# Norm weights loaded as rows and turned on TensorE, page-table loads issued by GpSimd, and the sync queue left to x and the projection weights

## What is computed

```
x      = 576 rows of 1024           (512 prompt rows, 64 sample rows)
xn     = x * rsqrt(mean(x*x) + eps) * attn_norm_g
q, k, v, qi, ki, wi, u, ga, gb = split(xn @ w_in)      # w_in: 1024 x 4168
ki     = rope(ki);  new_idx_k = ki
ki_all = [cache_idx_k[page_table], ki]                 # samples: 1024 cached keys, by pages of 128
score  = sum_h relu(qi . ki_all) * wi                  # then the best 128 or 256 keys of each query
o      = attention(q, k, v of the chosen keys)
pool_o = pooling branch of u, scaled by pool_scale
h      = x + (sig(ga) * (o @ W_ba) + sig(gb) * (pool_o @ W_bp)) @ w_out
h      = h + two experts of 32 for each token (RMSNorm with ffn_norm_g before it)
y      = RMSNorm_final(h)
```

## Time and profile before

| | |
|---|---|
| time, median of 3 runs | 1216.53 us (1213.72 to 1216.58) |
| profiled execution, first to last instruction | 1206.4 us |
| its own time | not listed apart: the median less the span is 10.1 us |
| PE busy | 1023.5 us, 85% |
| DVE, ACT, POOL busy | 352.1, 224.8, 172.1 us |
| mean rate of the DMA engines | 234 GB/s |
| mean granted TensorE clock | 0.938 |

### The profile page before, as it was taken

The page is one execution under the profiler, slowest core; times in us unless marked ns, Lnnn a source line. Parts: engine busy times, 40 slices in busy tenths (PEclk is TensorE's granted clock), DMA queues, the critical chain, the costliest instruction groups (busy, mean ns, idle before and its releaser), DMA issues.

```text
span 1206.4 us, 11854 instructions
## 1 busy us (share of the span) xinstructions
PE 1023.5 (85%) x4516; PEld 551.9 (46%) x4516; DVE 352.1 (29%) x754; ACT 224.8 (19%) x478; POOL 172.1 (14%) x257
## 2 busy tenths in 40 slices
PE   3998999999999999999985798878888788777780
PEld 3543444767776565775552334333333333333330
DVE  1048999973332111231233001000000000000006
ACT  4144211223333223200221011001100111001002
POOL 2732451100000120000134101000000000000012
PEclk9999999899999999999996799888997999988995
DMA  6420022421201341953035999999999999999986
GB/s 221 172 70 1 7 90 85 166 81 39 71 1 70 140 154 63 369 230 140 17 122 192 331 357 391 400 397 406 404 401 403 400 405 405 395 399 408 396 357 215
DMA packets 51038, 282.66 MB, mean 234 GB/s; under 512 B 12232, under 2 KB 12952, under 8 KB 36143
## 3 DMA queue, kind: packets, MB, share of 16 engines
q1 hardware_dynamic: 37287, 237.82, 51.0%
q0 software_dynamic: 8592, 35.92, 8.5%
q10 hardware_dynamic: 5120, 8.39, 1.8%
HBM read 267.37 MB, written 14.79 MB: 234 GB/s over the span
## 4 chain that ended last, share of the span: by engine, by line
PE 61%; DVE 18%; issue 8%; DMA 5%; ACT 4%; SPq 2%; POOL 1%; another core or an unknown queue 0%; POOLq 0%; ACTq 0%; DVEq 0%
PE psum L952 19%; PE psum L967 10%; PE psum L729 8%; DVE arena L1354 6%; DVE arena L1352 6%; PE psum L875 5%; PE psum L567 3%; PE psum L857 3%; PE psum L811 2%; PE psum L743 2%; PE psum L762 2%; DVE arena L1567 2%; DMA arena<-in_w_branch_pool 2%; PE psum L960 2%; ACT arena L1244 1%
## 5 line engine op out<-in xcount | busy, mean ns | idle before, releaser
L952 PE MATMUL psum<-arena 128*64 128x512 f32 x1024 | 248.2, 640 | 57.7 <-issue 56.9
L952 PEld LDWEIGHTS psum<-arena 128*64 128x64 f32 x1024 | 88.6, 148 | 214.7 <-issue 214.7
L967 PE MATMUL psum<-arena 128*64 128x512 f32 x512 | 130.8, 656 | 17.7 <-ACT arena L1248 17.7
L729 PE MATMUL psum<-arena 128*128 128x288 f32 x480 | 125.3, 408 | 0.0
L567 PE MATMUL psum<-arena 128*128 128x512 f32 (+2 forms) x320 | 120.4, 537 | 2.1 <-ACT arena L1113 2.1
L1567 DVE TENSOR_TENSOR arena<-arena,psum 64x512 f32<-64x512 f32 x32 | 22.1, 690 | 304.3 <-ACT arena L1244 304.3
L729 PEld LDWEIGHTS psum<-arena 128*128 128x128 f32 x480 | 89.2, 190 | 28.0 <-issue 5.4
L1244 ACT ACTIVATE arena<-psum 64x512 f32<-64x512 f32 x32 | 18.9, 590 | 436.6 <-PE psum L952 426.6
L567 PEld LDWEIGHTS psum<-arena 128*128 128x128 f32 (+1 forms) x320 | 58.0, 209 | 54.7 <-issue 51.7
L967 PEld LDWEIGHTS psum<-arena 128*64 128x64 f32 x512 | 44.1, 149 | 80.7 <-issue 80.7
L1571 DVE COPY arena<-psum 128x512 f32<-128x512 f32 x32 | 22.1, 692 | 182.5 <-PE psum L967 182.5
(11 more groups left out here) (235 smaller groups left out, 959.4 us busy)
## 6 DMA issues: line engine op xcount, KB each, us to landing
arena<-in_w_exp_down SPq DMA_DIRECT2D x32, 2048.0 KB, 24.3
arena<-in_w_exp_gate SPq DMA_DIRECT2D x31, 2048.0 KB, 18.6
arena<-in_w_exp_up SPq DMA_DIRECT2D x30, 2048.0 KB, 24.6
arena<-in_w_in SPq DMA_DIRECT2D x8, 2048.0 KB, 9.1
y_d<-arena ACTq DMA_DIRECT2D x64, 128.0 KB, 8.3
arena<-in_x_prompt SPq DMA_DIRECT2D x8, 512.0 KB, 6.6
arena<-in_w_out SPq DMA_DIRECT2D x2, 2048.0 KB, 8.0
arena<-in_w_exp_up SPq DMA_DIRECT2D x4, 1024.0 KB, 20.5
```

What stands on the lines that cost most here:

```text
L729: last = pe.matmul(bank(2 + n % 2 if n < SAMPLE_G else 2, HN), ring[slot % 2][:, k, m * P:(m + 1) * P], xnT[:, k, HN * hh:HN * hh + HN], s ...
L952: last = pe.matmul(bank(2 + s, 512, slice(64 * half, 64 * half + 64)), xT[s][:, k, :], w, start=(k == 0), stop=(k == KD - 1))
L967: last = pe.matmul(bank(4 + s, 512, slice(64 * half, 64 * half + 64)), hT[s][:, k, :], wd[s][:, k, 512 * half:512 * half + 512], start=(k ...
```

## The change

Three vectors of weights are loaded as 20 rows of 128 neighbouring numbers into a small tile `grow`, by ACT in place of SP. PE transposes the tile ahead of everything else into 20 columns of bank 2, and DVE copies them into `stats`; the wait of DVE for the vectors moves from behind its first two reciprocals to ahead of them. The eight page-table loads are issued by POOL as its first work. SP issues two tiles of x, then `kiww`, then the other three tiles of x, and goes on to the ring.

```diff
+        grow = at(SMALL, P, rows=20)
...
-            for i in range(TILES):
+            def load_x(i):
                 sp.dma_start(xin[i][0:rows_of(i), :], x_rows[i]).then_inc(s_x[i], 16)
-            with nc.allow_non_contiguous_dma(reason="a few small columns"):
-                for j in range(NPAGE):
-                    src = page_table[:, j:j + 1].rearrange("b j -> j b").to_broadcast([GR, DB])
-                    sp.dma_start(pgi[GR * j:GR * (j + 1), :], src).then_inc(S["page_in"], 16)
-                sp.dma_start(gain1, attn_norm_g[0].rearrange("(k p) -> p k", p=P)).then_inc(S["gain_in"], 16)
-                sp.dma_start(pscale, pool_scale[0].rearrange("(k p) -> p k", p=P)).then_inc(S["gain_in"], 16)
-                sp.dma_start(gain2, ffn_norm_g[0].rearrange("(k p) -> p k", p=P)).then_inc(S["gain_in"], 16)
-                sp.dma_start(kiww, w_in_v[:, :, C_KI:C_KI + KIW]).then_inc(S["kiww_in"], 16)
+
+            load_x(0)
+            load_x(1)
+            sp.dma_start(kiww, w_in_v[:, :, C_KI:C_KI + KIW]).then_inc(S["kiww_in"], 16)
+            load_x(2)
+            load_x(3)
+            load_x(4)
...
             pe.wait_ge(S["const_in"], 16)
+            pe.wait_ge(S["gain_in"], 48)
+            pe.transpose(bank(2, 20), grow, ident[0:20, 0:20]).then_inc(S["gain_in"], 1)
...
+            for row, g in ((0, attn_norm_g), (8, ffn_norm_g), (16, pool_scale)):
+                n = g.shape[1] // P
+                act.dma_start(grow[row:row + n, :], g[0].rearrange("(k p) -> k p", p=P)).then_inc(S["gain_in"], 16)
             act.wait_ge(S["st_ready"], 1)
...
+            dve.wait_ge(S["gain_in"], 49)
+            link(dve.tensor_copy(stats[:, 0:20], bank(2, 20)))
             inverse_rms(0)
             inverse_rms(1)
-            dve.wait_ge(S["gain_in"], 48)
...
+            with nc.allow_non_contiguous_dma(reason="the page table, a column for each page"):
+                for j in range(NPAGE):
+                    src = page_table[:, j:j + 1].rearrange("b j -> j b").to_broadcast([GR, DB])
+                    pool.dma_start(pgi[GR * j:GR * (j + 1), :], src).then_inc(S["page_in"], 16)
             pool.wait_ge(S["gi_ready"], 1)
```

## The result

The changed kernel takes 1219.4 us (median of 20 runs, 1209.89 to 1222.19), the kernel before 1214.2 us in the same sessions. The ratio is 1.0035, with a 95% interval from 1.0019 to 1.0050: slower by 2.3 to 6.1 us, where 8.1 us less were forecast. Comparisons leave disturbed runs out.

What follows compares the result with a forecast made beforehand. The opening was taken as bound by the wait for the last weight vector, not by an engine. Terms -7.1 and -1.0 sum to -8.1, from 1216.5 to 1208.4 us, range 1205.5 to 1212.5.

Steps and rivals of the forecast that it cites:

- The first wait and its price: In the opening, T1 on PE waits for the last vector of weights; removing that gives at most 8.8 us.
- engines that were not full: there was idle time in them to be filled: DMA share of 0.10 in 9:17 read as room for other loads, so more than issuing time is saved.
- a tenth for the other queues' packets: Allowance for other queues' packets beside x, moving T1's start from 13.0 to 13.1.
- the term of -7.1 us: T1 on PE starts at 13.1 instead of 20.22, the largest term of the sum.
- The 1212.1 that the prediction drew from this rule: Alternative time in us if spreading loads over issuing engines saves only the page table's issue, 4.42 us; not adopted.
- kiww ahead of the third tile, 1.5 us: In SP's queue, kiww before x's third tile delays that tile by 1.5 us, so T1 moves from 11.46 to 13.0.
- Vectors, 0 to +0.5: Before T0: loading by ACT, transpose and copy fit idle time; first scaling in time or late by some tenths.
- Page table on POOL, needed by 16.5: Loads land by 10.1, 1.09 us apart; no cost up to 16.5, then one for one.
- The two rivals built on it: Page table late, taking turns with x: 1211.5 us, chance 0.18; very late, loads waiting for each other: 1226.4, chance 0.06.
- The slower one: Page table lands at 34.5, 18.0 behind need, at 4.2 us a load: 1226.4 us, chance 0.06.
- From T1 on, -1.0: Behind T1, products P3 and P4 get back part of PE's clock missing in 35:40: 1.0 us less.
- The opening reaches the end whole: Time gained in the opening shortens the whole kernel equally, as later busy stretches hold no wait for a time.

Runs made afterwards that it cites:

- e_row_again: The same kernel as e_row_hold, measured again beside the kernel before; ratio 0.9937.
- e_beside: e_row_hold's kernel plus eight unread POOL loads beside x, each 128 single numbers from different addresses of a weight vector; ratio 0.9941 to the kernel before.
- e_row_hold: Changed kernel with the page table as one load of 8 rows by ACT, spread on chip, POOL's gathers waiting for x; ratio 0.9903 to the kernel before.
- e_pages_sp: Changed kernel with the eight page-table loads back on SP's queue, behind x; ratio 0.9959 to the kernel before.
- e_pages_hold: Changed kernel in which POOL issues the page-table loads only when all of x has landed; ratio 1.0034 to the kernel before.
- e_pages_twice: Changed kernel with eight more page-table loads on POOL, into a place nobody reads; ratio 1.0058 to the kernel before.
- e_row_free: e_row_hold's kernel without POOL's wait for x ahead of its gathers; ratio 0.9938 to the kernel before.
- e_probe: e_row_hold's kernel plus 32 extra unread small loads of four kinds on SP's queue behind x; one execution only, no ratio.
- e_row_columns: e_row_hold's kernel with the three vectors again as 2560 single numbers on SP's queue behind x; ratio 0.9947 to the kernel before.

## Why the prediction was wrong

*The first wait and its price*: right. The vectors were what T1 waited for, the gap between 11.46 and 20.22 was real, and e_row_again gives back 8.4 us of it.

*"engines that were not full: there was idle time in them to be filled"*: this is the step that failed. I read the share of 0.10 in 9:17 as free engines and concluded that the page table's loads would stop hurting once out of x's queue; I charged x "a tenth for the other queues' packets". In the changed kernel the share was low too (0.33 in 9:17), and x waited all the same: a low share is time in which no packet is counted, not time that another queue can have. Measured, the third square moved by 11.1 us, not by 1.6, and the term of -7.1 us came out as +2.4. The Trainium skill's page "DMA: Bandwidth & Descriptors", section "Issuing engines are not separate DMA queues", says that all issuing engines' transfers interleave on the same 16 DMA engines. The trace agrees in so far as a queue of its own bought nothing (third square 20.01). The 1212.1 that the prediction drew from this rule is still a gain: interleaving as such, seen with small loads of other addresses in e_beside, cost x only 1.6 us.

*kiww ahead of the third tile, 1.5 us*: mis-sized both ways. 0 us on the third square with nothing slow beside it, since ACT's own work up to there covers the later landing (8.99 and 8.95; 9.28 and 9.35), and 8.8 us on the third square beside the page-table loads (20.01 and 11.20).

*Vectors, 0 to +0.5*: the copy was done by 6.3, ahead of the need. Right. T0 came 1.9 us late (11.05), but for the second tile of x and not for the vectors.

*Page table on POOL, needed by 16.5*: it landed last at 20.3, at 1.86 us a load and not 1.09, but x was later still, so this wait never showed. The two rivals built on it had the right loads and looked at the wrong victim: they priced the table as late, and left x alone. The slower one had the sign right, with 9.9 us where 2.3 to 6.1 were measured; as its mechanism did not occur, that is luck.

*From T1 on, -1.0*: it did not come in the changed kernel. From T1 to the keys took 31.3 us before and 31.2 after. In e_row_again it was 29.7 and in e_row_hold 30.1, about the forecast's size.

*The opening reaches the end whole*: right within what can be told. The three best openings, 9.1 to 9.9 us shorter, measured 7 to 12 us less. For e_pages_sp, e_pages_hold and e_pages_twice the ratios of the times lie 3 to 6 us below what the keys of their profiles say. In each of the three the profiled execution was the slowest of the ten, so the profile shows more delay than the median run has.

What else stays open: how a slow read keeps the other queues' packets from an engine was not observed, only that they move less beside it and by how much. And in several profiles DVE waits 2 to 5 us for a TensorE record that is long over, as at 27.92 in the earlier trace rows. There the record of T3's first half ends at 30.28 and its semaphore counts up only at 32.94; no run isolated why.

## What to carry to other kernels

A load that is slow while the DMA engines count as idle is not harmless, and moving it to another queue can move the harm onto the stream beside it. Ask first why it is slow: here 16 partitions read the same few addresses; one read of the whole table, 8 rows of 32 bytes, spread on chip by a copy and a transpose, took the whole cost away. Look in the trace, too, whether an experiment ran what it was made for: in e_row_free the second stream moved nothing until the first was all but over. And price a reordering for the queue as it will be: the same `kiww` cost nothing in a free queue and 9 us in a creeping one.

## What the runs showed of the hardware

- 128 single integers for 16 partitions from the same 8 addresses of the page table take 1.09 us a load, 128 single numbers from different addresses of a weight vector about 0.1, on the same queue (e_probe: 132 and about 1400 packets in a microsecond; the kernel before: 122 and 1860).
- Beside a stream the same page-table loads take 1.86 us each.
- Beside such loads on POOL's queue the DMA engines moved 158 (5 to 11 us) and 102 GB/s (9 to 17 us), beside those on ACT's queue 224 and 232, and beside loads of the same shape from spread addresses 316 and 308.
- A low DMA share is compatible with engines that have nothing to give: 0.33 with x waiting.
- 2560 single numbers from spread addresses in three loads behind x cost 2.2 us on the path (e_row_columns).
- POOL's gathers, issued from 8.50 us on, moved no packet before 14 us (e_row_free).
